# A mixture of experts on Trainium2: the high and low rows of the experts' first product in one stationary tile

## What is computed

```python
def expert_block(args):
    xblk, e = args
    hdn = jax.nn.silu(xblk @ w1[e]) * (xblk @ w3[e])
    return hdn @ w2[e]
```

## Time and profile before

| What | us |
|---|---|
| Median of 3 runs | 2409.75 |
| Lowest, highest run | 2396.01, 2411.46 |
| Profiled execution, span from first to last instruction | 2405.5 |
| Expert stage, about | 1652 to 2329 of the span |

### The profile page before, as it was taken

How to read it: one execution, slowest core, us unless ns; L and a number is a source line. 1 busy time by engine, 2 the same in 40 slices (tenths; PEclk the granted TensorE clock), 3 DMA queues, 4 the chain that set the end, 5 groups by cost and what they waited for, 6 DMA issues and landing times. The chain is left out here.

```text
span 2405.5 us, 29813 instructions
## 1 busy us (share of the span) xinstructions
PE 2048.6 (85%) x11254; PEld 1783.3 (74%) x11254; DVE 1020.0 (42%) x1064; ACT 886.1 (37%) x1080; POOL 267.6 (11%) x306
## 2 busy tenths in 40 slices
PE   6999999999899995777859979924999999999960
PEld 6999999999899994333459977813777777777750
DVE  5000010122222001545553433264777777777745
ACT  5122211121212112544230003212766777777742
POOL 0000000000000001211100000014121111111113
PEclk9999999999999997666779989956999999999985
DMA  4322253333955412233165345323998888998967
GB/s 149 112 74 72 77 152 123 108 103 103 211 140 145 87 68 94 74 112 112 56 232 164 110 157 180 136 114 107 349 349 332 341 338 329 351 344 340 342 213 243
DMA packets 180758, 435.63 MB, mean 181 GB/s; under 512 B 37553, under 2 KB 116081, under 8 KB 156113
## 3 DMA queue, kind: packets, MB, share of 16 engines
q1 hardware_dynamic: 151984, 340.14, 41.4%
q0 software_dynamic: 23584, 77.75, 10.1%
q10 hardware_dynamic: 5120, 16.78, 1.8%
HBM read 347.52 MB, written 94.97 MB: 184 GB/s over the span
## 5 line engine op out<-in xcount | busy, mean ns | idle before, releaser
L1272 DVE TENSOR_TENSOR WL<-RAW,WH 128x2048 fp32r<-128x2048 f32 x34 | 77.9, 2292 | 623.9 <-ACT WH L949 623.9
L1642 DVE TENSOR_TENSOR E1L<-E,E1H 128x2048 fp32r<-128x2048 f32 x128 | 292.7, 2288 | 68.8 <-ACT E1H L1163 68.6
L1163 ACT ACTIVATE E1H<-E 128x2048 fp32r<-128x2048 f32 x128 | 244.7, 1914 | 98.5 <-DMA E<-in_exp_w_dram 98.2
L1775 PE MATMUL ps<-XH,WH 128*128 128x384 f32 (+1 forms) x1176 | 263.3, 332 | 11.7 <-issue 7.7
L1775 PE MATMUL ps<-XL,WH 128*128 128x384 f32 (+1 forms) x1176 | 260.7, 330 | 0.0
L1775 PE MATMUL ps<-XH,WL 128*128 128x384 f32 (+1 forms) x1176 | 260.3, 329 | 0.0
L1775 PEld LDWEIGHTS ps<-XH,WH 128*128 128x128 f32 x1176 | 201.4, 189 | 17.3 <-issue 13.5
L1738 PE MATMUL ps<-WH,XH 128*128 128x256 f32 x720 | 206.8, 287 | 5.3 <-ACT OT L957 2.0
L1738 PE MATMUL ps<-E1H,XTH 128*128 128x512 f32 x512 | 208.9, 408 | 2.5 <-DVE XTL L1657 2.5
L1739 PE MATMUL ps<-WL,XH 128*128 128x256 f32 x720 | 205.2, 285 | 0.0
L1740 PE MATMUL ps<-WH,XL 128*128 128x256 f32 x720 | 205.2, 285 | 0.0
(11 more groups left out here) (302 smaller groups left out, 3311.2 us busy)
## 6 DMA issues: line engine op xcount, KB each, us to landing
E<-in_exp_w_dram SPq DMA_DIRECT2D x192, 1024.0 KB, 7.2
RAW<-in_w_in_dram SPq DMA_DIRECT2D x34, 1024.0 KB, 5.6
feat<-OF POOLq DMA_DIRECT2D x24, 1088.0 KB, 4.6
yb<-YS ACTq DMA_DIRECT2D x64, 256.0 KB, 6.7
sg<-feat SPq DMA_DIRECT2D x24, 544.0 KB, 5.5
tokd<-OT POOLq DMA_DIRECT2D x10, 1024.0 KB, 5.3
cbuf<-feat SPq DMA_DIRECT2D x16, 544.0 KB, 6.1
yb<-yt POOLq DMA_DIRECT2D x3, 2816.0 KB, 18.5
```

The source lines that it names most:

```text
L1163: act.activation(E1H[st.s][:, i], E1[st.s][:, i], ACT.Copy).then_inc(e1_hi, 1)
L1272: dve.tensor_tensor(WL[st.s][:], RAW[st.s][:], WH[st.s][:].bitcast(F32), ALU.subtract).then_inc(wl_ready, 1)
L1642: dve.tensor_tensor(E1L[st.s][:, i], E1[st.s][:, i], E1H[st.s][:, i].bitcast(F32), ALU.subtract).then_inc(e1_lo, 1)
L1775: last = pe.matmul(ps[:, 3 * f + g, 0:tn], w[:, k, :], x[:, k, t0:t0 + tn], start=(k == 0 and i == 0), stop=(k == nk - 1 and i == 2))
```

## The change

The high and low half of the block's rows now stand side by side in one stationary tile `XS`: columns 0 to 63 are the high half, columns 64 to 127 the low half, where zeros stood before. The first product is then two matmuls a slice instead of three: `XS` over `E1H` and `XS` over `E1L`. Rows 0 to 63 of the PSUM bank hold the share of the high half, rows 64 to 127 that of the low half (the product low x low is now included). They have to be added: ScalarE copies rows 64 to 127 to `hb` at partitions 0 to 63 (`low_rows`), and VectorE adds `hb` to rows 0 to 63 of the bank into `hs` (`h_add`), 64 x 512 each. `silu` and `hidden` read `hs` instead of PSUM. ScalarE's turn becomes ..., `y_out`, `low_rows` of k, `x_hi` of k+1, `silu` of k, `split2` of k; VectorE's ..., `low1`, `h_add` of k, `x_lo` of k+1, `hidden` of k. So `silu` now also stands behind `x_hi`. Four memsets before barrier 5 go. The output projection's four load semaphores are taken from those of an earlier phase (`wo_in`), with their counts moved; this frees names and changes no order.

```diff
-        XTH = [sb(f"XTH{i}", [P, KD, P], F32R) for i in range(2)]
-        XTL = [sb(f"XTL{i}", [P, KD, P], F32R) for i in range(2)]
+        XS = [sb(f"XS{i}", [P, KD, P], F32R) for i in range(2)]
+        hb = sb("hb", [BR, 2 * DE])
+        hs = sb("hs", [BR, 2 * DE])
...
             def x_hi(st):
                 act.wait_ge(xg_tp, st.n + 1)
-                act.activation(XTH[st.s][:, :, 0:BR], ps[:, 0, :].rearrange("p (k t) -> p k t", k=KD), ACT.Copy).then_inc(xth, 1)
-
-            def silu(st):
+                act.activation(XS[st.s][:, :, 0:BR], ps[:, 0, :].rearrange("p (k t) -> p k t", k=KD), ACT.Copy).then_inc(xth, 1)
+
+            def low_rows(st):
                 act.wait_ge(h_mm, st.n + 1)
                 if not (st.first and st.s == 0):
+                    act.wait_ge(h_sum, st.n)
+                act.activation(hb[:], ps[BR:P, 2 + st.s, :], ACT.Copy).then_inc(h_low, 1)
+
+            def silu(st):
+                act.wait_ge(h_sum, st.n + 1)
+                if not (st.first and st.s == 0):
                     act.wait_ge(h_ready, st.n)
-                act.activation(sil[:], ps[0:BR, 2 + st.s, 0:DE], ACT.Silu).then_inc(h_sig, 1)
+                act.activation(sil[:], hs[:, 0:DE], ACT.Silu).then_inc(h_sig, 1)
...
-                silu(st)
+                low_rows(st)
                 if more:
                     x_hi(nxt)
+                silu(st)
                 if not (st.first and st.s == 0):
                     split2(st)
...
-            for b in XTH + XTL + [HTH, HTL]:
+            for b in (HTH, HTL):
                 dve.memset(b[:, :, BR:].bitcast(F32), 0.0)
...
-                dve.tensor_tensor(XTL[st.s][:, :, 0:BR], ps[:, 0, :].rearrange("p (k t) -> p k t", k=KD), XTH[st.s][:, :, 0:BR].bitcast(F32), ALU.subtract).then_inc(xtl, 1)
+                dve.tensor_tensor(XS[st.s][:, :, BR:], ps[:, 0, :].rearrange("p (k t) -> p k t", k=KD), XS[st.s][:, :, 0:BR].bitcast(F32), ALU.subtract).then_inc(xtl, 1)
+
+            def h_add(st):
+                dve.wait_ge(h_low, st.n + 1)
+                if not (st.first and st.s == 0):
+                    dve.wait_ge(h_sig, st.n)
+                dve.tensor_tensor(hs[:], ps[0:BR, 2 + st.s, :], hb[:], ALU.add).then_inc(h_sum, 1)
...
-                dve.tensor_tensor(hid[:], ps[0:BR, 2 + st.s, DE:2 * DE], sil[:], ALU.mult).then_inc(h_ready, 1)
+                dve.tensor_tensor(hid[:], hs[:, DE:2 * DE], sil[:], ALU.mult).then_inc(h_ready, 1)
...
-                hidden(st)
+                h_add(st)
                 if more:
                     x_lo(nxt)
+                hidden(st)
...
                 for k in range(KD):
-                    last = three(ps[:, 2 + s, :], XTH[s][:, k, :], XTL[s][:, k, :], E1H[s][:, :, k, :], E1L[s][:, :, k, :], k == 0, k == KD - 1)
+                    pe.matmul(ps[:, 2 + s, :], XS[s][:, k, :], E1H[s][:, :, k, :], start=(k == 0), stop=False)
+                    last = pe.matmul(ps[:, 2 + s, :], XS[s][:, k, :], E1L[s][:, :, k, :], start=False, stop=(k == KD - 1))
                 last.then_inc(h_mm, 1)
```

More of the change, by code:

```diff
@@ L360, in trunk @@
         sg_in, mix_ready, mix_st = sem("gate_in"), sem("mix_ready"), sem("mix_stored")
-        wo_in, wo_hi, wo_lo, m_in, m_hi, m_lo = [sem(f"wo_in{i}") for i in range(4)], sem("wo_hi"), sem("wo_lo"), sem2("mix_in"), sem("mix_hi"), sem("mix_lo")
+        wo_in, WO_IN0 = z_in[1:], 16 * 3
+        wo_hi, wo_lo, m_in, m_hi, m_lo = sem("wo_hi"), sem("wo_lo"), sem2("mix_in"), sem("mix_hi"), sem("mix_lo")
         r4_in, o_mm, x2_ready, x2_rms, n2_ready, n2_tp, n2_tc, l_mm, l_ready = (
@@ L371, in trunk @@
         e1_hi, e1_lo, e2_hi, e2_lo = sem("e1_hi"), sem("e1_lo"), sem("e2_hi"), sem("e2_lo")
+        h_low, h_sum = sem("e_h_low_rows"), sem("e_h_summed")
         xg_tp, xth, xtl, h_mm, h_sig, h_ready, h_tp, hth, htl, y_mm, y_ready = (
@@ L1121, in hi_wo @@
             def hi_wo(i):
-                act.wait_ge(wo_in[i], 16)
+                act.wait_ge(wo_in[i], WO_IN0 + 16)
                 act.activation(WOH[:, 2 * i:2 * i + 2, :], WOR[:, 2 * i:2 * i + 2, :], ACT.Copy).then_inc(wo_hi, 1)
```

## The result

| | before | after |
|---|---|---|
| Median, 4 runs each | 2406.28 us | 2424.68 us |
| Lowest, highest | 2396.01, 2411.46 | 2421.94, 2432.61 |
| Ratio to before, 95% interval | | 1.0088 [1.0055, 1.0121] |
| Profiled execution: time, span | span 2405.5 | 2422.09, span 2420.2 |

The changed kernel does a third less matmul work in the experts' first product and is 0.9% slower. The view to start from is again the expert stage's busy times, with the same columns as the earlier trace rows: TensorE, its weight loads, VectorE, ScalarE, GpSimd, then the clock, the DMA share and GB/s.

A forecast was written before the change was run, and what follows sets the result against it. It took the loop of expert weight loads as the bound, TensorE just beneath. 30 periods x 0.95 = 28.5 us, less 5 at the ends, 23.5 on the span of 2405.5, plus 4.25: 2433 us; range 2402 to 2460.

The forecast's parts named there:

- the loop of loads: Expert stage: weight load, `E2H`, `E2L`, next load; 20.82 us per two experts, 11.0 of transfer and 10.2 of work.
- The landing turn: The turn in which ScalarE waits for w3's load: `E2H` 0.95 us later, all on the loop, bounds 0.64 and 1.63.
- The product turn: The turn whose load is there in time and Silu waits for TensorE: `E2H` 0.52 us later, counted as nothing.
- its ring: VectorE and ScalarE waiting on each other in a turn: 6.80, `h_add` 0.68, Silu 0.28, `E2H` 1.90 and hand-overs, 9.75 us.
- TensorE's saving: Expert first product: 8 of 24 matmuls fewer, 1.87 us a turn, worth nothing on the loop in the landing turn.
- the ends: First experts and last product of the stage, where TensorE sets the pace: 3 and 2 us gained.
- TensorE as the bound: Rival, expert stage: TensorE sets the pace, periods fall from 20.8 to 19.5 us, 44 off, 2366 us; chance 10%.
- The loads give it back: Rival, w3's load: later issues meet an emptier queue and hide the added 0.95 us; 2405, or 2419 by half; 27%.
- The clock: Rival, TensorE in the stage: wider gaps bring 1.2 GHz and both turns count; 2449 us, at worst 2463; 18%.

The follow-up runs named there:

- the move of `E2H` and `E2L`: Both put ahead of the second half of the next expert's w1/w3, in ScalarE's wait for w3: 2369.00 us on the changed kernel, 2386.92 us on the kernel before.
- the doubled sum: The changed kernel with `h_add` run twice, the first time into a tile that nobody reads: 2450.41 us, ratio 1.0192.
- Silu out of the ring: The changed kernel with `E2H` and `E2L` moved, then Silu and `hidden` moved into the next turn and `split2` ahead of `h_hi`: 2461.79 us, ratio 1.0232.

## Why the prediction was right, and where it was off

**The bound.** The prediction read the loop of loads as the bound and TensorE as second, just beneath. Both hold: the move of `E2H` and `E2L` gave 17 us in the kernel before, where TensorE then set the pace at 20.07, and 56 in the changed one.

**The new instructions.** Predicted: `hb` 0.59, `hs` 0.68. The groups of the changed kernel in the stage, count, then busy us and mean ns of one, then idle time before:

```profile
L1757 PE MATMUL ps<-E2H,HTH 128*128 128x512 f32 x216 | 107.5, 498 | 83.6 <-ACT YS L1199 83.2 <-DVE HTL L1684 0.4
...
L1674 DVE TENSOR_TENSOR hs<-ps,hb 64x512 f32<-64x512 f32 x54 | 36.7, 681 | 0.3
...
L1187 ACT ACTIVATE hb<-ps 64x512 f32<-64x512 f32 x54 | 32.1, 595 | 42.3 <-ACT YS L1199 39.8 <-PE ps L2029 2.5
```

0.595 and 0.681. The interpolation between rows of the same engine was good enough.

**The landing turn.** Predicted +0.90 from the rows and +0.95 with an allowance for the hand-over; measured +0.90 where the slot is the same, in the timeline and in the means. The step is right, and the allowance was not needed.

**The product turn.** Predicted 9.75 for its ring and nothing on the period. Two of its `E2L` stand 9.8 apart above, and the doubled sum shows that the product turn's share is hidden.

**The term that was off** is TensorE's saving: "On the loop this buys nothing in the landing turn", and so nothing in the sum but at the ends. It is worth 0.27 to 0.34 us a period, 8 to 10 us over the stage. That is the gap between the predicted period, 21.7 to 21.8, and 21.43, and between the span's forecast growth, 23.5, and the measured 14.7. (Of the 8 us between 2433 and 2424.68 some 3.5 are the base: the median before was taken as 2409.75 and is 2406.28 with the fourth run.) That ScalarE doesn't wait for TensorE in the landing turn was read rightly; the saving comes by the other side of the loop, where w3's load lands some 0.3 sooner after its issue. The forecast had the load's time unchanged. What makes it land sooner stays open.

The wait for YS grew:

```profile
PE ps L1757 <- ACT YS L1199: 83.2, 38, 4.2
...
ACT sil L1193 <- DVE hs L1674: 8.7, 15, 0.8
```

The longest is 4.2 us, which the prediction had worked out as some 4 for every period; the mean of the 38 is 2.2. And ScalarE's wait for `hs` before Silu, foreseen for every turn, hardly shows as idle time (8.7 us in all), since `x_hi` fills it. TensorE's busy time was to fall by 1.87 a turn, some 100 us over the stage's 54 turns; it fell by 72.8, with the matmuls of the second product longer than before (next paragraph).

**The rivals.** TensorE as the bound: false here, true for the kernel before once the move is made. The loads give it back: false for the sum, which makes w3's load no shorter (10.58 and 10.72 with three matmuls, 10.27 and 10.36 with two), and the doubled sum came through whole. It is the missing matmul that goes with shorter loads. The clock: it fell as foreseen, from 0.99 to 0.91 (0.92 was forecast), in most periods with a part at 1.2 GHz. The matmuls of the second product, behind the gap, were before (busy us and mean ns of one stand behind the first bar):

```profile
L1738 PE MATMUL ps<-E2H,HTH 128*128 128x512 f32 x221 | 93.2, 422 | 15.7 <-ACT YS L1190 15.6
```

Their mean went from 422 to 498 (the group of L1757 above); 69 of the 216 took 0.6 us or more, before 6 of 221. The rule of the Trainium skill, "TensorE: Matmul & The Clock Gate", section "HAM oscillation", that waits for data between groups of matmuls send the clock to half, agrees with this in the changed kernel, but not each wait does it here: with Silu out of the ring TensorE waits 2.24 us a turn and the stage's clock is 0.95. That the lower clock would make the kernel slow is not borne out: with the clock back at 0.98 and the third matmul in, the kernel is slower, not faster.

## What to carry to other kernels

Look for the loop that holds the period: load, the work up to the buffer's release, next load. What stands in it cost one to one here, by its length on the path (0.9 of work for 0.93 to 1.00 of period); an engine that is 97% busy but not in the loop paid back under a tenth of the 3.7 us a period saved on it. Ask first whether the work between landing and release can be taken out by order alone: here that was worth three times what the change had cost, and turned the change from a loss into a gain.

## What the runs showed that was not expected

- A DMA share of 0.97 at 357 GB/s over the stage was not the limit of the time: with 307 GB/s the same kernel took the same 2370 us.
- A third matmul whose result is ready before it is read in the landing turn still cost 0.27 to 0.34 us a period, and the time showed not as a wait for TensorE but as a load of w3 that took some 0.3 longer to land.
- With the move, all periods last the same to 0.1 us; before, they went from 19.6 to 22.8 us. The spread lay in the loop over the loads, not in the engines.
- The sustained rate was 357 and 354 GB/s in the two kernels with the move. The prediction set a stretch of 4 us at 397 against the limit of about 358 that the Trainium skill, "DMA: Bandwidth & Descriptors", section "Where 436 GB/s comes from", gives. The stretch from 1700 to 2280 takes in the end of the loads; from 1700 to 2240 the changed kernel with the move holds 361. From the page's figure the prediction estimated that no period could fall below 19.8 us; that kernel's last 19.64. So the rates of these runs lie near the page's figure, and the highest slightly above it. Both kernels are held by engines, so none of the runs shows that figure as a bound, nor how far above it a rate could go.
